# A causal mask on VectorE in PSUM instead of a product with the identity on TensorE

## The reference

```python
def forgetting_attention(q, k, v, log_f):
    for i in range(S // Q_BLOCK):                 # 4 blocks of 128 queries
        q0 = i * Q_BLOCK
        kend = q0 + Q_BLOCK
        s = jnp.einsum('bqhd,bkhd->bhqk', qf[:, q0:kend], kf[:, :kend]) * scale
        bias = c[:, :, q0:kend, None] - c[:, :, None, :kend]
        mask = (q0 + jnp.arange(Q_BLOCK))[:, None] >= jnp.arange(kend)[None, :]
        s = jnp.where(mask, s + bias, -jnp.inf)
        p = jax.nn.softmax(s, axis=-1)
        outs.append(jnp.einsum('bhqk,bkhd->bqhd', p, v[:, :kend]))
```

## Time and profile before

| | us |
|---|---|
| median of 3 runs | 1093.13 |
| lowest and highest | 1092.72, 1093.31 |
| the profiled execution | 1092.22 |
| its span, first to last instruction | 1090.5 |
| TensorE busy in it | 1073.1 |
| VectorE busy | 667.7 |
| ScalarE busy | 503.1 |
| granted clock of TensorE, share of full speed | 0.999 |

### The profile page before, as it was taken

How to read it: one execution, slowest core, us unless ns; L and a number is a source line. 1 busy time by engine, 2 the same in 40 slices (tenths; PEclk the granted TensorE clock), 3 DMA queues, 4 the chain that set the end, 5 groups by cost and what they waited for, 6 DMA issues and landing times.

```text
span 1090.5 us, 15968 instructions
## 1 busy us (share of the span) xinstructions
PE 1073.1 (98%) x6526; PEld 956.5 (88%) x6526; DVE 667.7 (61%) x809; ACT 503.1 (46%) x728; POOL 44.6 (4%) x96
## 2 busy tenths in 40 slices
PE   7999999999999999999999999999999999999997
PEld 5899999998888978888888888889899999988886
DVE  6788888873334663476664333468787787753334
ACT  7355455452223583667774222344444554542222
POOL 2000000000001310001000000011000000000001
PEclk9999999999999999999999999999999999999999
DMA  9522422424232544332115335315424234253311
GB/s 289 193 78 78 154 79 80 153 96 175 96 81 59 163 120 115 88 78 78 40 39 154 97 101 169 97 39 174 154 87 146 79 103 130 78 176 114 96 40 78
DMA packets 116099, 121.16 MB, mean 111 GB/s; under 512 B 6560, under 2 KB 100784, under 8 KB 116032
## 3 DMA queue, kind: packets, MB, share of 16 engines
q1 hardware_dynamic: 112960, 115.47, 34.2%
q10 hardware_dynamic: 2096, 2.10, 0.9%
q0 software_dynamic: 976, 2.66, 0.7%
HBM read 111.80 MB, written 6.29 MB: 108 GB/s over the span
## 4 chain that ended last, share of the span: by engine, by line
PE 85%; DVE 6%; ACT 3%; issue 2%; DMA 2%; POOL 1%; SPq 1%; ACTq 0%; DVEq 0%; POOLq 0%
PE bank L1418 25%; PE bank L1504 11%; PE bank L1505 11%; PE bank L1506 11%; PE bank L1408 6%; PE bank L1410 6%; PE bank L1409 6%; PE bank L1626 1%; PE bank L1627 1%; PE bank L1628 1%; DVE w_lo L923 1%; PE bank L1473 1%; PE bank L1475 1%; PE bank L1474 1%; DMA raw<-in_ffn_w_up 1%
## 5 line engine op out<-in xcount | busy, mean ns | idle before, releaser
L1504 PE MATMUL bank<-tc,w_hi 128*128 128x256 f32 x576 | 163.2, 283 | 0.0
L1505 PE MATMUL bank<-tc,w_hi 128*128 128x256 f32 x576 | 163.0, 283 | 0.0
L1506 PE MATMUL bank<-tc,w_lo 128*128 128x256 f32 x576 | 163.0, 283 | 0.0
L923 DVE TENSOR_TENSOR w_lo<-raw,w_hi 128x1024 fp32r<-128x1024 f32 x72 | 87.7, 1221 | 97.9 <-ACT w_hi L524 97.8
L1418 PE MATMUL bank<-w_hi,a_hi 128*128 128x512 f32 x408 | 126.1, 390 | 0.0
L1418 PE MATMUL bank<-w_lo,a_hi 128*128 128x512 f32 x408 | 125.7, 389 | 0.0
L1418 PE MATMUL bank<-w_hi,a_lo 128*128 128x512 f32 x408 | 125.6, 389 | 0.0
L1408 PE MATMUL bank<-u_hi,w_hi 128*128 128x512 f32 x312 | 123.8, 397 | 0.2 <-issue 0.2
L1504 PE MATMUL bank<-u_hi,w_hi 128*128 128x256 f32 x432 | 122.4, 283 | 1.3 <-DVE scr L1050 1.3
L1037 DVE TENSOR_TENSOR w_lo<-raw,w_hi 128x1024 fp32r<-128x1024 f32 x36 | 44.1, 1225 | 129.3 <-ACT w_hi L602 129.3
L1505 PE MATMUL bank<-u_lo,w_hi 128*128 128x256 f32 x432 | 122.3, 283 | 0.0
(11 more groups left out here) (242 smaller groups left out, 2063.0 us busy)
## 6 DMA issues: line engine op xcount, KB each, us to landing
raw<-in_w_in SPq DMA_DIRECT2D x40, 512.0 KB, 3.8
raw<-in_ffn_w_down SPq DMA_DIRECT2D x36, 512.0 KB, 3.6
raw<-in_ffn_w_gate SPq DMA_DIRECT2D x10, 1024.0 KB, 5.4
raw<-in_ffn_w_up SPq DMA_DIRECT2D x10, 1024.0 KB, 8.5
h<-in_ffn_w_gate SPq DMA_DIRECT2D x8, 1024.0 KB, 5.5
h<-in_ffn_w_up SPq DMA_DIRECT2D x8, 1024.0 KB, 8.7
raw<-in_ffn_w_up SPq DMA_DIRECT2D x8, 512.0 KB, 4.3
h<-in_x SPq DMA_DIRECT2D x8, 512.0 KB, 6.9
```

The costliest lines, as they stand in the source:

```text
L923: V.tensor_tensor(w_lo[:, slot(u), :], raw[:, slot(u), :], w_hi[:, slot(u), :].bitcast(F32), ALU.subtract).then_inc(lo_ready, 1)
L1504: mm(dst, w_hi[:, slot(u), w], moving(n, 0, k), start=first and k == 0, stop=False, skip_group_check=True)
L1505: mm(dst, w_hi[:, slot(u), w], moving(n, 1, k), start=False, stop=False, skip_group_check=True)
L1506: last = mm(dst, w_lo[:, slot(u), w], moving(n, 0, k), start=False, stop=k == KD // 2 - 1, skip_group_check=True)
```

## The change

The product with the identity goes. The second product of the scores ends the group and counts `scores_ready`. VectorE then adds the tile `causal` (now plain float32) to the last 128 columns of the scores in PSUM, counts a new semaphore `scores_masked`, waits for it, and takes the maximum as before. The tile `ident_r` and its cast at the start go.

```diff
-        ident_r = sb("ident_r", [P, P], F32R)
-        causal = sb("causal", [P, P], F32R)
+        causal = sb("causal", [P, P])
...
+        scores_masked = sem("scores_masked")
...
-            V.tensor_copy(ident_r[:, :], ident[:, :])
             V.tensor_copy(causal[:, :], arena[:, 0, 0:P])
...
                     dve.wait_ge(scores_ready, sl + 1)
+                    diagonal = bank[:, B_S[sl % 2], kend - P:kend]
+                    V.tensor_tensor(diagonal, diagonal, causal[:, :], ALU.add).then_inc(scores_masked, 1)
+                    dve.wait_ge(scores_masked, sl + 1)
                     V.tensor_reduce(neg_max[:, sl:sl + 1], bank[:, B_S[sl % 2], 0:kend], AX.X, ALU.max,
                                     negate=True).then_inc(max_ready, 1)
...
                     mm(dst, heads_of(p, QS[e])[:, toks], heads_of(p, KH[e])[:, 0:kend], start=True, stop=False)
-                    mm(dst, second_query(p, e)[:, toks], heads_of(p, KL[e])[:, 0:kend], start=False, stop=False)
-                    mm(dst[:, qb * P:kend], ident_r[:, :], causal[:, :], start=False, stop=True).then_inc(scores_ready, 1)
+                    mm(dst, second_query(p, e)[:, toks], heads_of(p, KL[e])[:, 0:kend], start=False, stop=True).then_inc(scores_ready, 1)
```

## The result

The changed kernel took **1097.0 us** (median of five runs, 1096.8 to 1098.7) against 1092.7 us before, measured side by side: a ratio of 1.0043, 95% interval [1.0032, 1.0054]. It is slower by 4.3 us; the forecast was 3.9 us more, to the same 1097.0, from a median of 1093.1. The profiled execution of after is 1097.53 us, its span 1095.8.

The account below looks back on a forecast made before the run. Two close limits were seen in attention: TensorE and the ScalarE-VectorE exchange. Terms -1.04 + 1.8 + 1.6 + 0.3 + 1.2 = 3.9 us took 1092.22 to 1096.1; 0.9 for the median gave 1097.0 us, range 1093.0 to 1099.0.

Parts of the forecast that it names:

- What bounds the kernel: Attention stage, 431 to 558 us: two close limits, TensorE and the ScalarE-VectorE exchange of one block, step after step.
- Rival (a): Whole attention stage: TensorE is the bound, so all 3.7 us are won, 1089.4 us; chance 0.10.
- rival (b): Attention stage: gain and cost cancel, 8 or 10 masks on the path instead of 17, 1091 to 1095.3 us; chance 0.18.
- m: Cost of one mask, the addition on VectorE plus its own wait: 0.32 us, bounds 0.289 to 0.42.
- Rival (c): Addition into PSUM much dearer, 0.5 us, with more masks on the path: some 8 us slower, 1101 us; chance 0.06.
- The prices: Attention stage: each removed TensorE product saves 0.115 us, each mask added on VectorE costs 0.32 us.
- Slots 0 to 8: Attention steps until 462.90 us: masks covered by ScalarE's waits for TensorE, nine removed products win time, -1.04 us.
- Slots 9 to 18: Attention steps from 462.90 to 507.42 us: five masks on the path plus 0.2 leaking through, 5m + 0.2 = +1.8 us.
- Slots 19 to 24: Attention steps to 527.58 us: six masks on the path less some 0.3 us of play, 6m - 0.3 = +1.6 us.
- pass the delay of four masks on: Around maximum 22: VectorE waits for TensorE, but ScalarE's squares have no such wait, so four masks' delay goes through.
- Slots 25 and 26: Attention steps to 537.53 us: mask 25 covered by ScalarE's wait, mask 26 on the path, m = +0.3 us.
- 27 to 31: Attention steps to 557.71 us: five masks on the path less 0.37 us of ScalarE's waiting, 5m - 0.37 = +1.2 us.

Follow-up runs that it names:

- covered: Kernel before with the addition on VectorE only in 15 slots (0 to 8, 10, 12, 16, 17, 18, 25), TensorE's product in the others: 1091.25 us, 0.9992.
- on the path: Kernel before with the addition on VectorE only in 17 slots (9, 11, 13 to 15, 19 to 24, 26 to 31), TensorE's product elsewhere: 1098.45 us, 1.0056.
- the path alone: Kernel before, TensorE's product kept, with the addition on VectorE on top in slots 9 to 18 only: 1094.23 us against 1092.28, 1.0019.

## Why the prediction was right, point by point

**What bounds the kernel.** Right. The kernel without a mask (-1.75 us of a possible 3.7) and the pair "covered" and "on the path" show it. Rival (a), TensorE as the bound, and rival (b), 8 to 10 masks on the path, fall. The last product with the values is 3.64 + 1.95 = 5.59 us later in the kernel with idle products than in the kernel without a mask, both profiles without a fall; that is 17 times m. Rival (c), a dear addition, falls with the row of 291 ns.

**The prices.** One product of TensorE: 0.115 predicted, 0.11 measured. One mask: 0.32 predicted, 0.325 measured. The own wait costs 0.034 us beyond the 291 ns, as the chained rows had it, against the sentence of the Trainium skill that a semaphore between two operations costs nothing extra (VectorE: DVE Perf Modes, section The DRAIN you can't avoid). No run leaves the wait out, but operations on VectorE that don't need each other start some 0.07 us before the end of the one ahead (in the profile of before L923 runs from 509.33 for 1.21 us, and the maximum behind it starts at 510.47). The 291 ns themselves are what the formula of the Trainium skill gives (the same page, section on the TRN2 errata). The prediction's "below 3.4 us" for m = 0.29 is 3.43 by its own formula.

**Slots 0 to 8.** -1.04 predicted, -1.06 measured. The twofold addition shows that the cover there has an end: of nine second additions it lets 0.54 us through.

**Slots 9 to 18.** +1.8 predicted. Measured without a fall of the clock: +1.79 and +1.82 in the two kernels that keep TensorE's product; +0.75 running in the kernel with idle products, against 0.76.

**Slots 19 to 24.** The one mis-sized term: 6m - 0.3 = 1.6 predicted, 2.10 - 0.75 = 1.35 measured in the profile without a fall, and 1.34 to 1.36 in those of after, of both ways of masking, of the path alone and of the changed kernel again. The "some 0.3 us of play" at the start of the load were right: with idle products ScalarE's copy L860 comes 2.47 us late and TensorE's L1689 2.10, so 0.37. The step that failed is that ScalarE's squares "pass the delay of four masks on". Behind maximum 22, before and then with idle products:

```profile
519.42 0.69 DVE L1291 SCALAR_TENSOR_TENSOR arena<-scr,bank 128x512 f32<-128x512 f32 x1 [0.96 <-PE bank L1652]
...
522.20 0.69 ACT L794 ACTIVATE scr<-bank,neg_max 128x512 f32<-128x512 f32 x1
```

```profile
520.99 0.69 DVE L1293 SCALAR_TENSOR_TENSOR arena<-scr,bank 128x512 f32<-128x512 f32 x1 [0.32 <-ACT scr L809]
...
524.46 0.69 ACT L794 ACTIVATE scr<-bank,neg_max 128x512 f32<-128x512 f32 x1 [0.24 <-DVE neg_max L1280]
```

The exponential of slot 22 comes 2.08 us late, that of 23 2.13, that of 24 2.46. Mask 23 adds 0.05 us instead of 0.32: some 0.27 of the delay is absorbed between the two exponentials, so mask 23 belongs to the covered ones but for 0.05. The kernels without a mask and with early additions show the same play from the other side: their maxima are 1.06 us early up to slot 22 and 1.34 from slot 23 on.

**Slots 25 and 26; 27 to 31.** +0.3 predicted, +0.33 measured. +1.2 predicted, 3.64 - 2.43 = +1.21 measured.

**The sum.** Without falls of the clock it is 3.6 us at the last product with values, against 3.9 predicted. The prediction left out the falls, which in the profiled execution of after brought the shift to 4.9. In the medians, 4.0 us with idle products and 4.3 without, they are worth a few tenths, and 0.4 of the 4.0 is not accounted for by these points. The rise was therefore 3.9 predicted and 4.3 measured, with 0.3 too much in one term and more than that missing for the clock. That the time came out as 1097.0 to the tenth is luck: the prediction started from a median of 1093.1, and the kernel before took 1092.7 beside the changed one (1092.3 to 1092.5 in the later rounds), which makes up for just those 0.4 us. The range and the mechanism don't hang on it.

**What should have shown it.** The rows of the addition, of TensorE's pair of products, of ScalarE's waits (5 us more predicted, 5.8 measured) came as described, and behind 574 us the distance to before no longer grows (4.91, then 4.84). One did not: TensorE's waits in the stage should have grown by 6 to 7 us and grew by 4.6 only (from 1.8 to 6.4). That sum was short already: TensorE ends 3.9 us later with 3.7 us less to do, so by the prediction's own terms its waits grow by 7.6; the 1.04 us by which it was early at slot 9 were left out. The two falls, 3.4 us of lost speed, stand in the place of the rest: a slow TensorE arrives late where it would have waited. Its wait of 0.8 us for ScalarE's copy of slot 16 (L840), for example, is there in the three profiles of these additions that had no fall ahead of it, and is missing in after. A wait of 0.8 us at 555.67 for the gate's product on VectorE, new in after, was not foreseen; it swallows time that TensorE had won and moves nothing.

**Still open.** Why the clock falls behind a wait in one execution and not in the next. Ahead of slot 16, waits of 2.3 (twice) and 2.7 us had none behind them, one of 2.0 us (32 additions, 15 of them early) had; of two waits of 3.1 us one had and one had not.

## What to carry to other kernels

Where two engines hand a block to each other, an edit costs what stands on that path: count the instances that have no wait behind them to hide in, check each of them at the wait that follows it (mask 23 was counted and cost 0.05 us), and price those alone. Here 32 additions cost 6 us as they were placed and about 2 us where 15 of them stood in the adding engine's own wait (+0.3 against -1.75 without any). A product taken from an engine that is 98% busy wins only what is not in front of a wait that is there already.

## What the runs showed of the hardware

- A float32 addition over 128x128 that reads PSUM and SBUF and writes PSUM in place takes 291 ns on VectorE, the same as with its result in SBUF (289). A dependent operation behind a semaphore starts 0.03 us after its end.
- TensorE's granted clock fell to 0.50 behind waits of 1.2 to 3.4 us in five kernels, stayed low for some 3 to 7 us though the engine was busy again, and lengthened the start to start of 512 columns from 0.23 to 0.43 us. The same waits passed without a fall in other executions. A row of waits on a busy engine can thus cost more than its own length, by an amount that differs between executions.
